# Sums of squares in two rounded passes, two steps later, in a hybrid encoder layer on one core

## The reference, cut to what matters

```python
mod = jax.nn.silu(c) @ w_ada[l] + b_ada[l]
# queries and keys: head dimension 128, mean over it
q = rms_norm(q.reshape(B, S, ATT_HEADS, HEAD_DIM), q_norm_w)
q = apply_axial_rope(q, cos, sin) * (HEAD_DIM ** -0.5)
# output of the recurrent heads, 128 wide each
o = o[0] + flip(o[1])
o = rms_norm(o, out_norm_w) * jax.nn.silu(gate)
# rms_norm(x, w) = x * rsqrt(mean(x * x, axis=-1) + EPS) * w
```

## Time and profile before

| | us |
|---|---|
| median of 3 runs | 2377.59 |
| lowest and highest | 2376.49 and 2378.77 |
| span of the profiled execution | 2375.8 |
| TensorE busy in it | 2334.7 |
| VectorE busy | 1878.8 |
| ScalarE busy | 1104.8 |
| GpSimd busy | 128.6 |

### The profile page before, as it was taken

One profiled execution on the slowest core, in us unless ns is written; L12 is line 12 of the kernel. 1 busy time (PEld: TensorE's weight loads), 2 busy tenths in 40 slices (PEclk: granted clock), 3 DMA queues, 4 the chain that ended last, 5 costly groups with the idle time before them and its releaser, 6 DMA issues.

```text
span 2375.8 us, 37218 instructions
## 1 busy us (share of the span) xinstructions
PE 2334.7 (98%) x13671; PEld 2025.8 (85%) x13671; DVE 1878.8 (79%) x2447; ACT 1104.8 (47%) x1517; POOL 128.6 (5%) x207
## 2 busy tenths in 40 slices
PE   6999999999999999999999999999999999999998
PEld 3577778888888877878999999999999998888887
DVE  5875667887777873267799999999999998888777
ACT  4266744334443353254444444444444445555554
POOL 1010000000000000000000000000000000001100
PEclk9999999999999999999999999999999999999999
DMA  9952456666666734336555555555555559779966
GB/s 366 346 157 85 133 180 208 215 219 212 207 211 198 234 89 169 98 124 159 146 140 146 145 144 143 144 142 139 141 145 145 142 176 329 251 207 285 279 226 224
DMA packets 378834, 442.47 MB, mean 186 GB/s; under 512 B 14876, under 2 KB 295716, under 8 KB 376448
## 3 DMA queue, kind: packets, MB, share of 16 engines
q1 hardware_dynamic: 359056, 369.74, 49.1%
q0 software_dynamic: 19696, 71.68, 13.0%
HBM read 418.81 MB, written 66.08 MB: 204 GB/s over the span
## 4 chain that ended last, share of the span: by engine, by line
PE 87%; DVE 5%; DMA 3%; ACT 2%; issue 2%; SPq 0%; DVEq 0%; ACTq 0%
PE bank L2132 26%; PE bank L2134 26%; PE bank L2133 26%; DMA ADA<-in_w_ada_dram 2%; PE bank L2295 2%; DVE ACC L1373 2%; DMA AB_raw<-in_w_ada_dram 1%; PE bank L2198 1%; DVE ZZ L1577 1%; PE bank L2375 1%; PE bank L2314 1%; PE bank L2189 1%; DVE W_lo L1332 0%; PE bank L2063 0%; DVE AB_acc L1636 0%
## 5 line engine op out<-in xcount | busy, mean ns | idle before, releaser
L2132 PE MATMUL bank<-H_lo,W_hi 128*128 128x256 f32 (+1 forms) x1832 | 635.7, 347 | 0.0
L2134 PE MATMUL bank<-H_hi,W_lo 128*128 128x256 f32 (+1 forms) x1832 | 613.6, 335 | 0.0
L2133 PE MATMUL bank<-H_hi,W_hi 128*128 128x256 f32 (+1 forms) x1832 | 613.2, 335 | 0.0
L2132 PEld LDWEIGHTS bank<-H_lo,W_hi 128*128 128x128 f32 x1832 | 349.3, 191 | 35.8 <-issue 6.2
L2133 PEld LDWEIGHTS bank<-H_hi,W_hi 128*128 128x128 f32 x1832 | 349.3, 191 | 35.7 <-issue 6.2
L2134 PEld LDWEIGHTS bank<-H_hi,W_lo 128*128 128x128 f32 x1832 | 348.8, 190 | 35.6
L2132 PE MATMUL bank<-T_lo,W_hi 128*128 128x256 f32 x1280 | 362.2, 283 | 0.0
L2133 PE MATMUL bank<-MGR,W_hi 128*128 128x256 f32 x1280 | 362.2, 283 | 0.0
L2134 PE MATMUL bank<-MGR,W_lo 128*128 128x256 f32 x1280 | 362.2, 283 | 0.0
L2132 PEld LDWEIGHTS bank<-T_lo,W_hi 128*128 128x128 f32 x1280 | 245.8, 192 | 0.0
L2133 PEld LDWEIGHTS bank<-MGR,W_hi 128*128 128x128 f32 x1280 | 245.8, 192 | 0.0
(11 more groups left out here) (311 smaller groups left out, 3741.7 us busy)
## 6 DMA issues: line engine op xcount, KB each, us to landing
AB_raw<-in_w_ada_dram SPq DMA_DIRECT2D x128, 512.0 KB, 4.4
UB<-in_w_up_dram SPq DMA_DIRECT2D x100, 512.0 KB, 4.1
W_raw<-in_w_in_dram SPq DMA_DIRECT2D x90, 512.0 KB, 4.8
t_dram<-in_w_down_dram POOLq DMA_DIRECT2D x88, 512.0 KB, 8.1
DRAW<-in_w_down_dram SPq DMA_DIRECT2D x66, 512.0 KB, 5.8
W_raw<-in_w_up_dram SPq DMA_DIRECT2D x56, 512.0 KB, 3.9
ADA<-in_w_ada_dram SPq DMA_DIRECT2D x48, 512.0 KB, 9.0
W_raw<-in_w_down_dram SPq DMA_DIRECT2D x44, 512.0 KB, 6.1
```

The costliest lines, as they stand in the source:

```text
L2132: pe.matmul(acc, st_hi, mv_lo, start=start, stop=False, skip_group_check=on)
L2133: pe.matmul(acc, st_hi, mv_hi, start=False, stop=False, skip_group_check=on)
L2134: return pe.matmul(acc, st_lo, mv_hi, start=False, stop=stop, skip_group_check=on)
```

## The change

Queries' sums and those of the recurrent heads 0 to 6 are made from two rounded operands. ScalarE copies the square into a rounded part (`SQA_hi`, in the memory of `RSA`; `SQ_hi`, in that of `RS`), VectorE subtracts it from the square in place (`SQA_lo`, `SQ_lo`), and TensorE multiplies both by a rounded matrix of ones in two passes in place of one float32 product. The copy waits for the former head's last product. The keys' sums and that of the last recurrent head stay as they were. For queries the sum moves from step 1 to step 3 on TensorE, while ScalarE's Ln stays at its place in the order (step 2); the subtraction stands behind the rotation's addition on VectorE. For recurrent heads the sum moves from step 73 to 75, Ln and Exp from 74 to 76, the last product from 76 to 78. Both halves of the column sums come after step 79.

```diff
+    ones_r = at("ones_r", [P, P], F32R, C0 + 1024)
@@ ScalarE, query, step 0
                 act.activation(SQA[:, :], src, ACT.Square).then_inc(rope_in, 1)
+                if r >= KV_HEADS:
+                    if r == KV_HEADS:
+                        act.wait_ge(consts_landed, 16)
+                        act.activation(ones_r[:, :], ones[:, :], ACT.Copy)
+                    act.wait_ge(rope_in, rope_parts(r) + 1)
+                    act.wait_ge(rope_done, r)
+                    act.activation(SQA_hi[:, :], SQA[:, :], ACT.Copy).then_inc(rope_in, 1)
@@ ScalarE, recurrent head
                     act.activation(SQ[:, :], PB[4][:, :], ACT.Square).then_inc(o_squared, 1)
+                    if not (isinstance(p, int) and p == HG_HEADS - 1):
...
+                        act.activation(SQ_hi[:, :], SQ[:, :], ACT.Copy).then_inc(o_squared, 1)
-                if g == 74:
+                if g == (74 if isinstance(p, int) and p == HG_HEADS - 1 else 76):
                     act.wait_ge(o_summed, p + 1)
@@ VectorE, query, behind the addition
+                if r >= KV_HEADS:
+                    dve.wait_ge(rope_in, rope_parts(r) + 2)
+                    dve.tensor_tensor(SQA_lo[:, :], SQA[:, :], SQA_hi[:, :].bitcast(F32), ALU.subtract).then_inc(rope_in, 1)
@@ VectorE, recurrent head, step 73
                     dve.tensor_tensor(OG[:, :], PB[4][:, :], GW[:, :], ALU.mult).then_inc(o_gated, 1)
+                    if not (isinstance(p, int) and p == HG_HEADS - 1):
+                        dve.wait_ge(o_squared, p * 3 + 2)
+                        dve.tensor_tensor(SQ_lo[:, :], SQ[:, :], SQ_hi[:, :].bitcast(F32), ALU.subtract).then_inc(o_squared, 1)
-                if g == 76:
+                if g == (76 if isinstance(p, int) and p == HG_HEADS - 1 else 78):
@@ TensorE
-                pe.wait_ge(rope_in, r + 1)
+                pe.wait_ge(rope_in, rope_parts(r + 1))
...
+                    pe.matmul(PB[2][:, :], ones_r[:, :], SQA_hi[:, :], start=True, stop=False)
+                    pe.matmul(PB[2][:, :], ones_r[:, :], SQA_lo[:, :], start=False, stop=True).then_inc(rope_psum, 1)
             def att_side(h, s):
-                if s == 1:
+                if s == 3:
                     rope_mm(h + KV_HEADS)
...
+                    pe.matmul(PB[5][:, :], ones_r[:, :], SQ_hi[:, :], start=True, stop=False)
+                    pe.matmul(PB[5][:, :], ones_r[:, :], SQ_lo[:, :], start=False, stop=True).then_inc(o_summed, 1)
-                if g == 73:
+                if g == (73 if isinstance(p, int) and p == HG_HEADS - 1 else 75):
                     sum_squares(p)
-                    if g in (77, 78):
-                        sum_chunk(h, first and e == 0, g - 77)
+                    if g == 79:
+                        sum_chunk(h, first and e == 0, 0)
+                        sum_chunk(h, first and e == 0, 1)
```

More of the change, by code:

```diff
@@ L219, in hybrid_encoder_layer @@
     SQA = at("SQA", [P, S], F32, OV + 12 * KB)
+    SQA_lo = at("SQA_lo", [P, S], F32R, OV + 12 * KB)
     RSA = at("RSA", [P, S], F32, OV + 14 * KB)
+    SQA_hi = at("SQA_hi", [P, S], F32R, OV + 14 * KB)
     T1 = at("T1", [P, S], F32, OV + 16 * KB)
@@ L238, in hybrid_encoder_layer @@
     SQ = at("SQ", [P, S], F32, OV + 24 * KB)
+    SQ_lo = at("SQ_lo", [P, S], F32R, OV + 24 * KB)
     RS = at("RS", [P, S], F32, OV + 26 * KB)
+    SQ_hi = at("SQ_hi", [P, S], F32R, OV + 26 * KB)
     OG = at("OG", [P, S], F32, OV + 28 * KB)
@@ L388, in hybrid_encoder_layer, with rope_parts @@
         QR = [MX[:, 12 + n, :] for n in range(4)]
+        def rope_parts(r):
+            return r if r < KV_HEADS else KV_HEADS + 3 * (r - KV_HEADS)
         def q_bank(k):
@@ L842, in rope_rs @@
                 act.wait_ge(rope_psum, r + 1)
-                if r:
+                if 0 < r < KV_HEADS:
                     act.wait_ge(rope_done, r)
@@ L1018, in hg_side @@
                     act.activation(SQ[:, :], PB[4][:, :], ACT.Square).then_inc(o_squared, 1)
-                if g == 74:
+                    if not (isinstance(p, int) and p == HG_HEADS - 1):
+                        act.wait_ge(o_squared, p * 3 + 1)
+                        if not (isinstance(p, int) and p == 0):
+                            act.wait_ge(o_done, p)
+                        act.activation(SQ_hi[:, :], SQ[:, :], ACT.Copy).then_inc(o_squared, 1)
+                if g == (74 if isinstance(p, int) and p == HG_HEADS - 1 else 76):
                     act.wait_ge(o_summed, p + 1)
@@ L1617, in hg_side @@
                 if g == 73:
-                    dve.wait_ge(o_squared, p + 1)
+                    dve.wait_ge(o_squared, p * 3 + 1)
                     dve.tensor_tensor(OG[:, :], PB[4][:, :], GW[:, :], ALU.mult).then_inc(o_gated, 1)
-                if g == 76:
+                    if not (isinstance(p, int) and p == HG_HEADS - 1):
+                        dve.wait_ge(o_squared, p * 3 + 2)
+                        dve.tensor_tensor(SQ_lo[:, :], SQ[:, :], SQ_hi[:, :].bitcast(F32), ALU.subtract).then_inc(o_squared, 1)
+                if g == (76 if isinstance(p, int) and p == HG_HEADS - 1 else 78):
                     dve.wait_ge(o_gated, p + 1)
@@ L2157, in rope_mm @@
                     pe.wait_ge(att_out, r - KV_HEADS - 1)
-                pe.matmul(PB[2][:, :], ones[:, :], SQA[:, :], start=True, stop=True).then_inc(rope_psum, 1)
+                if r < KV_HEADS:
+                    pe.matmul(PB[2][:, :], ones[:, :], SQA[:, :], start=True, stop=True).then_inc(rope_psum, 1)
+                else:
+                    pe.matmul(PB[2][:, :], ones_r[:, :], SQA_hi[:, :], start=True, stop=False)
+                    pe.matmul(PB[2][:, :], ones_r[:, :], SQA_lo[:, :], start=False, stop=True).then_inc(rope_psum, 1)
             def turn_v(g):
@@ L2344, in sum_squares @@
             def sum_squares(p):
-                pe.wait_ge(o_squared, p + 1)
-                pe.matmul(PB[5][:, :], ones[:, :], SQ[:, :], start=True, stop=True).then_inc(o_summed, 1)
+                if isinstance(p, int) and p == HG_HEADS - 1:
+                    pe.wait_ge(o_squared, p * 3 + 1)
+                else:
+                    pe.wait_ge(o_squared, p * 3 + 3)
+                if isinstance(p, int) and p == HG_HEADS - 1:
+                    pe.matmul(PB[5][:, :], ones[:, :], SQ[:, :], start=True, stop=True).then_inc(o_summed, 1)
+                else:
+                    pe.matmul(PB[5][:, :], ones_r[:, :], SQ_hi[:, :], start=True, stop=False)
+                    pe.matmul(PB[5][:, :], ones_r[:, :], SQ_lo[:, :], start=False, stop=True).then_inc(o_summed, 1)
             def hg_side(p, g):
```

## The result

The changed kernel takes 2385.01 us (median of 13 runs, 2381.3 to 2388.72), the kernel before 2378.5 beside it (13 runs): a ratio of 1.0023, interval 1.0017 to 1.003. It is slower by 6.5 us. 2383.0 had been forecast, and slower by over 0.2% as the likeliest side.

A forecast was written before the change was run, and what follows sets the result against it. TensorE, busy 98% of the span, was taken to bound the kernel. Recurrent heads +2.5, level waits -0.5 and attention +3.4 gave +5.4 us on the profiled 2375.8, hence 2383.0 us as median, range 2376.5 to 2388.5.

The forecast's parts named there:

- recurrent term: Recurrent heads: passes saved, but Ln and Exp behind the weight copy make TensorE stand 1.08 us; +0.37 a head, +2.5 in all.
- the waits of the level: Merged-key waits in recurrent heads: earlier weight and modulation transfers may remove 1.9 us or meet worse; -0.5, ends -1.9 and +2.
- Price of the sums: On TensorE, two rounded passes cost 0.45 us, saving 0.42 in each of 15 sums, 6.3 us; one column-sum group saves 0.6.
- Rival (e): Sums on TensorE: new passes no faster than the old halves, up to +6.3 us, 2389; chance 3%.
- Head 0: First query: the sum waits for the subtraction behind the rotation, TensorE stands 1.85 us, scores come +2.4 us.
- Heads 5 to 7: Attention products already wait for Ln; the added copy moves Ln by 0.55 us, +1.65 for three heads.
- Heads 1 to 4: Attention products wait for Ln, gaining 0.17 us a head where the passes give 0.42; -0.7 for four.
- the landing: Recurrent heads: step 75's weight copy waits for a transfer issued at 471.35, landing at least 3.5 us later, not before 474.85.
- Rival (b): Recurrent heads: the weight copy doesn't hold Ln, TensorE stands 0.25 us, a head changes by -0.46; total 2377.2; chance 12%.
- Rival (d): Recurrent heads: modulation rows land late, each of seven heads waits 1 us more; +12, 2390; chance 11%.
- (c): Whole kernel: only TensorE's passes count since ScalarE has reserve, so 8.4 us go; 2369; chance 4%.
- (f): Recurrent heads: the exposed table switch on ScalarE has a drain, 1.38 us more a head; 2392.7; chance 2%.

The follow-up runs named there:

- fifth kernel: Queries' part of the change alone, with head 0's subtraction ahead of the rotation on VectorE, against the kernel before: 2379.85 us, ratio 1.0007.
- eighth kernel: Kernel before plus recurrent part, merged column sums in bank 7, and two passes for queries of attention heads 1 to 4 only, summed at step 2: 2372.33 us.
- third kernel: Kernel before with one edit, both halves of the column sums after step 79, all sums of squares still float32: 2383.19 us, ratio 1.0019.
- sixth: Recurrent part and merged column sums alone, with ScalarE's weight copy of step 75 moved to step 77, behind Exp, against the kernel before: 2384.56 us.
- second kernel: Only the recurrent heads' part and the merged column sums, queries as in the kernel before: 2381.13 us, ratio 1.0008.
- first: Only the queries' part of the change, recurrent heads and column sums as in the kernel before: 2382.15 us, ratio 1.0007.
- fourth: The second kernel with the column sums in bank 7, so they need not wait for Exp, against the kernel before: 2374.14 us, ratio 0.9975.
- ninth: The changed kernel with one edit, column sums in bank 7 without the wait for Exp, against the kernel before: 2376.47 us, ratio 0.9993.
- seventh: Kernel before with one edit, column sums in bank 7 without the wait for Exp, halves still after steps 77 and 78: 2374.63 us, ratio 0.9985.
- tenth: The eighth kernel with the column sums back in halves after steps 77 and 78, against the kernel before: 2370.51 us, ratio 0.9965.

## Why the prediction was right, and where its steps were not

**The total and its side were right, one half for the reasons given and the other by luck.** 2383.0 was forecast and 2385.01 measured, +5.4 forecast and +6.5 measured. The attention term held nearly line by line (+3.4 forecast, +3.8 or +3.9 found). The recurrent term had about the right size in the trace (+2.0 forecast with the waits of the level, +1.75 found), but by its passes and stands it was -2.7, and a clock that the forecast did not have brought it back. Nor does this account for the whole of the runs: 3.9 - 2.7 = +1.2, and the lower mean clock (0.9948 against some 0.9958) adds about 2 (an estimate from 1.5 us a stretch), where the means differ by 6.2, good to 1.7. Some 3 us are not traced.

**Price of the sums: right.** The two new passes stand 0.23 apart (480.96, 481.19), at the pitch of their neighbours. Rival (e) is out.

**Head 0: right, +2.4 for +2.4.** The fifth kernel shows the cause by its own removal: the subtraction behind the rotation is 1.7 of it.

**Heads 5 to 7: right, +0.57 for +0.55.** The passes are saved inside a wait that the added copy makes longer. The sixth head:

```profile
268.09 0.69 ACT L861 ACTIVATE RSA<-bank,SM 128x512 f32<-128x512 f32 x1
...
268.83 1.55 PE L2229 MATMUL bank<-PT,VSA 128*128 128x512 f32 x3 [1.27 <-ACT RSA L861]
```

**Heads 1 to 4: the right mechanism, too large by half.** -0.17 was forecast, -0.05 to -0.08 found. In the third head Ln starts behind the sum as worked out, and the product behind Ln:

```profile
207.61 0.69 ACT L861 ACTIVATE RSA<-bank,SM 128x512 f32<-128x512 f32 x1 [0.27 <-PE bank L2189]
208.36 1.98 PE L2229 MATMUL bank<-PT,VSA 128*128 128x512 f32 x4
```

The product starts 0.06 behind Ln's end, as forecast. What was left out is that a group which starts just behind the Ln that it waits for takes longer: in the kernel before, the group to the next pass took 3.14 us in the sixth head, which stood for Ln, and 3.03 in the third, where Ln had ended over 1 us earlier. -0.17 + 0.11 = -0.06. A stand is not needed for it. In the eighth kernel, with the sum a step earlier, the product of the third head starts 0.05 behind Ln's end with no idle time, and its group takes 3.14 as well:

```profile
202.95 0.69 ACT L864 ACTIVATE RSA<-bank,SM 128x512 f32<-128x512 f32 x1
```

```profile
203.69 3.70 PE L2232 MATMUL bank<-PT,VSA 128*128 128x512 f32 x8
```

Hence its 0.32 of the 0.42.

**Recurrent heads: the step that failed is the landing.** "In the trace the first table load is hidden", and Ln now comes behind the weight copy: right. The column sums start 3.79 behind the first sum pass in all seven heads, through that chain. But the copy was put at 474.85 + 0.02, behind a transfer that it does not need: the one issued at 471.35 is for the next unit, and step 75's own had landed at 470.2. In the changed kernel's third head the copy starts 1.2 us ahead of the landing of the transfer that the forecast named (552.29 against 553.5). So the landing's earliest, 3.5 us, its median and the 8.4 us between them never entered. The stand is 0.61 in place of 1.08, and a head changes by -0.10, not +0.37. The lower bound given, the end of the added copy, is what happened. Rival (b) had its condition, but not its result: with the transfer no longer last, Ln still stands behind the weight copy of 1.05 us and does not follow the sum, so a stand of 0.61 remains where (b) said 0.25.

**Waits of the level: right in kind.** The waits for merged keys went from 1.9 us to 0, the lower end of the term (by pitch it is 2.7 less, beyond that end). One sentence behind it was wrong: "The POOL queue has no step moved but by these shifts." POOL's transfers wait for step 79, which the merging puts ahead of the column sums; in the third kernel they come 2.1 us sooner by that alone. Rival (d), transfers that meet worse, did not come about in the changed kernel, but nothing in the forecast could have told how near it was. The third and sixth kernels have its mechanism, a row waited for 4 to 5 us in six heads, at +4.6 us over the kernel before and 4.4 more than the second kernel. What keeps the changed kernel clear is the order of the two issues, 1.85 us apart (482.74, 484.59).

**What was missing: the clock, and one stand.** Three more stretches of low clock, about 4.5 us in the profiled run, stand in no term, nor do the 0.8 us at the start of the last head. The profiles of all kernels, sorted by what stands ahead of the column sums in a recurrent head (the stretches are counted in one execution of each; means are over the runs, as differences from the kernel before of the same set, whose own clock is over all three sets):

| kernel | column sums | stand, us | low stretches in heads 1 to 6 | at the last head's start | mean, us | mean clock |
|---|---|---|---|---|---|---|
| changed | merged | 0.6 | 3 | 1 | +6.2 | 0.9948 |
| second | merged | 0.6 | 2 | 1 | +1.6 | 0.9947 |
| sixth | merged | 0.3 | 3 | 1 | +5.9 | 0.9946 |
| before | halves | 0.2 | 1 | 0 | 0 | 0.9958 |
| first | halves | 0.2 | 2 | 0 | +2.9 | 0.9958 |
| fifth | halves | 0.2 | 1 | 0 | +2.1 | 0.9954 |
| third | merged | 0 | 0 | 1 | +4.6 | 0.9960 |
| fourth | merged, bank 7 | 0 | 0 | 1 | -5.7 | 0.9960 |
| eighth | as the fourth | 0 | 0 | 1 (6.8 us long) | -6.1 | 0.9956 |
| ninth | merged, bank 7 | 0 | 0 | 1 (6.8 us long) | -1.9 | 0.9958 |
| seventh | halves, bank 7 | 0 | 0 | 0 | -4.0 | 0.9972 |
| tenth | halves, bank 7 | 0 | 0 | 0 | -8.2 | 0.9970 |

Two things come out, each without an exception. A low stretch inside the heads occurs only where TensorE stands ahead of the column sums, and then in 1 to 3 of the six heads, within 1.5 us of the end of the group. Three pairs of kernels that differ in the bank alone (second and fourth, changed and ninth, before and seventh) lose 2, 3 and 1 such stretches with the stand, and their mean clocks rise by 0.0010 to 0.0014. One at the last head's start occurs exactly where the sixteen products come in one group ahead of it. But there two things change together: in every merged kernel the first of TensorE's two stands there is 1.15 us or more (1.52 in the sixth), and 0.35 with the halves; the second, for VectorE's gate, is 0.88 or 0.89 in nine of the twelve. Whether the group or the longer stand brings the low clock, no run separates. The total of the stands does not: it is 1.35 us in the eighth kernel, which has the stretch, and 1.85 in the tenth, which has none.

The last head's start is also where the changed kernel loses most against before: the last of the seven stretches from head to head takes 75.25 us against 73.68. A stretch of low clock (1.5) and the longer stand (0.8) are in it, and the merged keys that waited before are out of it. So the change has two ways to a lower clock, and the prediction had neither. Changed against ninth is one bank apart, 8.1 us in the means. The stands are 4.3 of it and the return from a stand (0.08, as in the term of the sum) 0.6, which leaves 3.2 for the clock and all else; three stretches at 1.5 would be 4.5, but the ninth's one at the last head is longer. Why one head's stand is followed by a low stretch and another's equal one is not, these runs do not settle.

**Rivals (c) and (f).** (c), that the passes alone count, was out at once: TensorE waits for ScalarE or VectorE in every changed place but the recurrent sums. It is worth keeping in mind all the same, because with the waits taken away the fourth, eighth and tenth kernels reach toward it: the tenth has -8.2 us, near (c)'s 8.4, though a part of it is clock. (f) was wrong: the exposed switch takes 480.68 to 481.97, 1.29 us, with no drain. By the figure on the Trainium skill's page "ScalarE: Activation LUTs" ("What ACT_TABLE_LOAD costs"), 2.66 us a switch, the stand would have been 1.38 us more in each head, an estimate by that page. The measured rows decide against it.

## What to carry to other kernels

A faster instruction is worth its saving only where the engine that runs it goes on at once. Here 6.3 us of passes bought a copy and a subtraction in the chains of other engines, and in the traces the fifth kernel got part of the loss back, and the eighth three quarters of the saving, only by placing the step by the slack of each head rather than by one rule for all. Where an engine stands because two uses share a bank, ask first whether another bank is free: that edit alone gave 4.0 us before and 8.1 us after the change, where the arithmetic saves 6.3 us of passes at most. And when an instruction is moved in the order of a helper engine, work out which transfer it lets go, which of two buffers that transfer fills, and which other queue's transfers it must be ahead of.

## What the runs showed of the hardware that had not been expected

- Stretches of about 3.4 us at half the granted clock (1.2 of 2.4 GHz) come behind stands as short as 0.2 us (in the kernel before) of a TensorE that is otherwise busy; each costs some 1.5 us. The twelve profiles show them in the heads only with a stand. At the last head's start they come in the seven kernels with sixteen small products in one group and a first stand of 1.15 us or more, and not in the five with halves and a first stand of about 0.35.
- Three large transfers issued 1.3 us ahead by another queue delayed a modulation row: it landed after 9.3 to 10.2 us, and VectorE waited for it 26.4 us in six heads, 4.4 us each. Issued 0.83 us ahead of them, as in the kernel before, it landed after 4.4 or 4.5 us and was not waited for.
- A group of attention products that starts just behind the release it waits for takes about 0.1 us more than one whose release has long come (3.14 against 3.03 us), even where TensorE does not idle for it (203.69 in the eighth kernel).
